# A third buffer for evacuated projection tiles, later head transposes in layer two, and a new order in the first seven-product pair

## The reference

```
h += 0.5 * g1 * SwiGLU_1(mod(norm(h)))
h += g2 * W_out [ A window attention | B global attention with QK norm | C 2-D Fourier ] (mod(norm(h)) W_in)
h += 0.5 * g3 * SwiGLU_2(mod(norm(h)))
```

## Time and profile before

| what | value |
|---|---|
| median of 3 runs | 2603.0 us (2598.9 to 2603.01) |
| the profiled execution's own time | 2601.57 us |
| its span in the trace | 2599.5 us |
| TensorE busy | 2514.5 us, 97% |
| VectorE busy | 1948.2 us, 75% |
| ScalarE busy | 1149.9 us, 44% |
| GpSimd busy | 788.7 us, 30% |

### The profile page before, as it was taken

The page is one execution under the profiler, slowest core; times in us unless marked ns, Lnnn a source line. Parts: engine busy times, 40 slices in busy tenths (PEclk is TensorE's granted clock), DMA queues, the critical chain, the costliest instruction groups (busy, mean ns, idle before and its releaser), DMA issues.

```text
span 2599.5 us, 40233 instructions
## 1 busy us (share of the span) xinstructions
PE 2514.5 (97%) x14986; PEld 2308.1 (89%) x14986; DVE 1948.2 (75%) x3213; ACT 1149.9 (44%) x2131; POOL 788.7 (30%) x614
## 2 busy tenths in 40 slices
PE   7999999999988999999999999999999999899998
PEld 4999999988777899999999899999997787899997
DVE  5888788766498488788755888887567596877776
ACT  5533433443376262433444624333444474544443
POOL 1222121224187231221222312221323285333332
PEclk9999999999999999999999999999999999999999
DMA  6244445214430124444312244443123431133332
GB/s 247 98 149 138 130 130 155 78 57 159 102 90 1 57 83 131 134 141 147 114 57 74 86 134 131 137 146 114 62 66 115 118 78 49 61 94 98 102 106 82
DMA packets 132001, 276.16 MB, mean 106 GB/s; under 512 B 15584, under 2 KB 35296, under 8 KB 130528
## 3 DMA queue, kind: packets, MB, share of 16 engines
q1 hardware_dynamic: 131808, 273.60, 34.1%
HBM read 260.43 MB, written 13.11 MB: 105 GB/s over the span
## 4 chain that ended last, share of the span: by engine, by line
PE 79%; DVE 12%; ACT 4%; issue 3%; DMA 1%; POOL 0%; SPq 0%; ACTq 0%; DVEq 0%; POOLq 0%
PE ring L1839 38%; PE ring L1941 21%; PE ring L1952 14%; DVE wlo L1435 2%; DVE ptl L1259 1%; DVE neg_max L1236 1%; PE row L1760 1%; ACT pth L1098 1%; PE row L1775 1%; PE ring L1795 1%; DVE xl L1546 1%; DVE tl L1345 1%; DVE t_lat L1539 1%; ACT whi L946 1%; DVE prob L1249 1%
## 5 line engine op out<-in xcount | busy, mean ns | idle before, releaser
L1435 DVE TENSOR_TENSOR wlo<-raw,whi 128x512 fp32r<-128x512 f32 (+2 forms) x672 | 512.4, 773 | 302.9 <-ACT whi L946 302.2
L946 ACT ACTIVATE whi<-raw 128x512 fp32r<-128x512 f32 (+2 forms) x672 | 399.1, 605 | 383.3 <-PE ring L1941 240.8
L1839 PE MATMUL ring<-xh,whi 128*128 128x384 f32 (+1 forms) x1280 | 411.8, 322 | 0.7 <-DVE rstd L1414 0.7
L1839 PE MATMUL ring<-xl,whi 128*128 128x384 f32 (+1 forms) x1280 | 411.4, 321 | 0.0
L1839 PE MATMUL ring<-xh,wlo 128*128 128x384 f32 (+1 forms) x1280 | 411.2, 321 | 0.0
L1839 PE MATMUL ring<-th,whi 128*128 128x384 f32 (+1 forms) x960 | 313.6, 327 | 14.1 <-DVE acc L1300 8.4
L1839 PE MATMUL ring<-th,wlo 128*128 128x384 f32 (+1 forms) x960 | 312.1, 325 | 0.0
L1839 PE MATMUL ring<-tl,whi 128*128 128x384 f32 (+1 forms) x960 | 311.9, 325 | 0.0
L636 POOL TENSOR_TENSOR raw<-raw,s_two 128x512 f32<-128x512 f32 x80 | 116.2, 1452 | 618.9 <-DVE wlo L1435 577.3
L1442 DVE SCALAR_TENSOR_TENSOR ada_junk<-ada_tile,row 128x1024 bf16<-128x1024 f32 x256 | 301.5, 1215 | 0.0
L622 POOL TENSOR_TENSOR s_one<-raw 128x512 f32<-128x512 f32 x80 | 104.9, 1311 | 551.8 <-DMA raw<-w_gu 441.4
(11 more groups left out here) (218 smaller groups left out, 5489.4 us busy)
## 6 DMA issues: line engine op xcount, KB each, us to landing
raw<-w_gu SPq DMA_DIRECT2D x352, 256.0 KB, 3.1
ada_tile<-w_turned SPq DMA_DIRECT2D x130, 512.0 KB, 3.7
raw<-w_down SPq DMA_DIRECT2D x96, 256.0 KB, 3.6
raw<-w_down SPq DMA_DIRECT2D x64, 192.0 KB, 2.5
raw<-w_in SPq DMA_DIRECT2D x48, 256.0 KB, 3.4
raw<-w_down SPq DMA_DIRECT2D x64, 128.0 KB, 2.1
raw<-w_out SPq DMA_DIRECT2D x32, 256.0 KB, 8.5
ada_first<-w_first SPq DMA_DIRECT2D x4, 1536.0 KB, 13.7
```

Source lines behind the costliest of these rows:

```text
L946: act.activation(weights(q, 0, cols)[0], src[:, 0:cols], ACT.Copy).then_inc(whi_ready, 1)
L1435: dve.tensor_tensor(w_l, src[:, 0:cols], w_h.bitcast(F32), ALU.subtract).then_inc(wlo_ready, 1)
L1839: last = pe.matmul(out, w, x, start=(start and k == 0 and m == 0), stop=(k == HALF - 1 and m == 2), skip_group_check=not start)
```

## The change

Three things are done. (1) `un` becomes three buffers; the third lies in memory that the value tiles use later. ScalarE evacuates tile j before it rounds tile j - 2 (except for the last two roped tiles), and new waits on the finished rope guard the buffers on ScalarE and VectorE. (2) In layer two TensorE turns the head norms before step k = 6 and not k = 4. (3) In the first seven-product pair banks b and c change places, the third turned sum is rounded (ScalarE) and its rest taken (VectorE) later, behind the last weight splits of pair 1, and the waits of TensorE move to the blocks that need them; in the last feed-forward (`rounds_late`) the product of the pair before is rounded behind the third bank copy, and its rest taken behind one more weight split.

```diff
--- before.py
+++ after.py
@@ -299,7 +299,7 @@
         rot = sb("rot", [P, 2, SEQ], F32, work + 30720)
         ucos = sb("ucos", [P, 2, SEQ], F32, work + 34816)
         rope_tab = sb("rope_tab", [P, 2, SEQ], F32, work + 38912)
-        un = sb("un", [P, 2, TOK], F32, work + 43008)
+        un = [sb(f"un{i}", [P, TOK], F32, at_un) for i, at_un in enumerate((work + 43008, work + 46080, work + 6144))]
         uf = sb("uf", [P, 2, TOK], F32, work + 49152)
         pos_lat = sb("pos_lat", [P, 4, SEQ + 1], F32, work + 55296)
         pos_ctx = sb("pos_ctx", [P, 2, CTX + 1], F32, work + 63520)
@@ -409,7 +409,8 @@
         def pair_banks(i, w2):
-            return ring[pair_ring(i)][:, 0:w2], ring[0][:, 512:512 + w2], ring[1][:, 512:512 + w2]
+            a, low, high = ring[pair_ring(i)][:, 0:w2], ring[0][:, 512:512 + w2], ring[1][:, 512:512 + w2]
+            return (a, high, low) if i == PLAIN else (a, low, high)
         def weights(q, a, b):
@@ -432,6 +433,11 @@
             return s["sums"] + d + 1 + (KD - 1 - s["whole"] if p == 1 and d >= s["whole"] else 0)
+
+        def rounds_late(s):
+
+
+            return s["width"] == SEQ
         def even_odd(a):
@@ -705,7 +711,7 @@
                         if q >= 2:
                             pool.wait_ge(qlo_done, g - 1)
                         if width == TOK:
-                            pool.tensor_copy(roped[:, sl, SEQ:TOK], un[:, sl, SEQ:TOK])
+                            pool.tensor_copy(roped[:, sl, SEQ:TOK], un[q % 3][:, SEQ:TOK])
                         pool.tensor_tensor(rot[:, sl], rot[:, sl], rope_tab[:, 1], ALU.mult).then_inc(rope_done, 1)
                         pool.wait_ge(rope_done, 2 * g + 1)
                         pool.tensor_tensor(roped[:, sl, 0:SEQ], rot[:, sl], ucos[:, sl], ALU.add).then_inc(rope_done, 1)
@@ -782,13 +788,15 @@
                     act.activation(four[:].rearrange("p c n -> p (c n)"), bank[0][:, 0:4 * P], ACT.Copy).then_inc(four_ready, 1)
                 if j == UF[1]:
                     round_values(0)
-                if 0 <= j - 2 < ROPED:
+                if j - 2 in (ROPED - 2, ROPED - 1):
                     round_qk(j - 2)
                 act.wait_ge(piece_used, s["tile"][j] + 2)
                 if j in UF:
                     act.activation(uf[:, j % 2, 0:width], ring[j % 2][:, 0:width], ACT.Copy).then_inc(evac_done, 1)
                 else:
-                    last = act.activation(un[:, j % 2, 0:width], ring[j % 2][:, 0:width], ACT.Copy, scale=SCALE if j in QA else 1.0)
+                    if j >= 3:
+                        act.wait_ge(rope_done, 2 * (q0 + j - 3) + 2)
+                    last = act.activation(un[j % 3][:, 0:width], ring[j % 2][:, 0:width], ACT.Copy, scale=SCALE if j in QA else 1.0)
                     if j not in (KB,) + QB:
                         last.then_inc(evac_done, 1)
                     else:
@@ -798,6 +806,8 @@
                     if j == QB[2] + 1:
                         head_std(QB[2])
                         act.preload_act_table(ACT.Exp)
+                if 0 <= j - 2 < ROPED - 2:
+                    round_qk(j - 2)
             round_values(1)
         def act_fourier(act, layer, between):
@@ -826,6 +836,7 @@
             end = stages[n + 1]["first"] if n + 1 < len(stages) else len(plan.pieces)
             w2, done = width // 2, t_before(n)
             shift = MODC * layer + (6 if s["kind"] == "ffn2" else 0) * KD
+            round_late = rounds_late(s)
             def ahead(q):
@@ -877,11 +888,11 @@
             ahead(q)
             round_turned(0)
             ahead(q + 1)
-            round_turned(2)
             round_turned(1)
             plain_silu(1)
             ahead(q + 2)
             ahead(q + 3)
+            round_turned(2)
             open_pair = 1
             for unit in s["units"][PLAIN:]:
                 if len(unit) == 2:
@@ -904,15 +915,17 @@
                 if k > 0:
                     act.wait_ge(comb_done, 3 * k)
                 act.activation(m1[:, 0:w2], a_bank, ACT.Copy).then_inc(copy_done, 1)
-                if open_pair is not None:
+                if open_pair is not None and not round_late:
                     round_product(open_pair)
-                open_pair = i
                 ahead(q + 1)
                 act.wait_ge(piece_used, q + 2)
                 act.activation(m5[:, 0:w2], c_bank, ACT.Copy).then_inc(copy_done, 1)
                 ahead(q + 2)
                 act.wait_ge(piece_used, q + 3)
                 act.activation(u2[:, 0:w2], a_bank, ACT.Copy).then_inc(copy_done, 1)
+                if open_pair is not None and round_late:
+                    round_product(open_pair)
+                open_pair = i
                 if i == PLAIN:
                     round_turned(3)
                 ahead(q + 3)
@@ -1146,14 +1159,16 @@
                     if b == 0:
                         dve.wait_ge(qkg_ready, 1)
                     dve.wait_ge(head_spread, b + 1)
-                    dve.scalar_tensor_tensor(out=un[:, sl, 0:width], in0=un[:, sl, 0:width], scalar=qkg[:, kq:kq + 1],
+                    dve.scalar_tensor_tensor(out=un[j % 3][:, 0:width], in0=un[j % 3][:, 0:width], scalar=qkg[:, kq:kq + 1],
                                              in1=side[:, 0:width], op0=ALU.mult, op1=ALU.mult).then_inc(unorm_done, 1)
                     dve.wait_ge(unorm_done, b + 1)
                 dve.wait_ge(evac_done, e0 + j + 1)
                 if j == 0:
                     dve.wait_ge(tab_loaded, 16 * (layer + 1))
-                dve.stream_shuffle(rot[:, sl], un[:, sl, 0:SEQ], [i ^ 16 for i in range(32)])
-                dve.tensor_tensor(ucos[:, sl], un[:, sl, 0:SEQ], rope_tab[:, 0], ALU.mult).then_inc(rot_done, 1)
+                if q0 + j >= 2:
+                    dve.wait_ge(rope_done, 2 * (q0 + j - 2) + 2)
+                dve.stream_shuffle(rot[:, sl], un[j % 3][:, 0:SEQ], [i ^ 16 for i in range(32)])
+                dve.tensor_tensor(ucos[:, sl], un[j % 3][:, 0:SEQ], rope_tab[:, 0], ALU.mult).then_inc(rot_done, 1)
             def head_reciprocal(j):
@@ -1331,7 +1346,7 @@
                 parts = t_parts(s)
                 for p, (t1, c, a, b) in enumerate(parts):
-                    dve.wait_ge(thi_done, 4 * done + len(parts) * (0, 2, 1, 3)[x] + p + 1)
+                    dve.wait_ge(thi_done, 4 * done + len(parts) * x + p + 1)
                     v = t1.rearrange("p k (b e q) -> p k b e q", e=2, q=P)
                     src = (v[:, 0:HALF, :, 0], v[:, HALF:KD, :, 1], v[:, 0:HALF, :, 1], v[:, HALF:KD, :, 0])[x]
                     if x == 3:
@@ -1358,11 +1373,11 @@
             turned_sum(2)
             rest_turned(0)
             ahead(q + 1)
-            rest_turned(2)
+            rest_turned(1)
             ahead(q + 2)
-            rest_turned(1)
             product_rest(1)
             ahead(q + 3)
+            rest_turned(2)
             open_pair = 1
             for unit in s["units"][PLAIN:]:
                 if len(unit) == 2:
@@ -1395,10 +1410,12 @@
                 if i == PLAIN:
                     turned_sum(3)
                 ahead(q + 1)
-                if open_pair is not None:
+                if open_pair is not None and not rounds_late(s):
+                    rest_product(open_pair)
+                ahead(q + 2)
+                if open_pair is not None and rounds_late(s):
                     rest_product(open_pair)
                 open_pair = i
-                ahead(q + 2)
                 if i == PLAIN:
                     rest_turned(3)
                 ada_slot((n, *unit))
@@ -1630,6 +1647,11 @@
             blocks = 6 if x_w == TOK else 4
             e0 = W_IN_TILES * layer
+            def spread_at(layer):
+
+
+                return KD // 2 if layer < DEPTH - 1 else KD - 2
+
             def head_squares(j):
                 b, width = 4 * layer + j - KB, w_in_width(layer, j)
@@ -1657,7 +1679,7 @@
                     elif half == 0:
                         pe.wait_ge(four_ready, layer + 1)
                     for m in range(n_):
-                        last = pe.transpose(bank[half][:, m * P:(m + 1) * P], un[:, b, (a + m) * P:(a + m + 1) * P], ident[:])
+                        last = pe.transpose(bank[half][:, m * P:(m + 1) * P], un[(VA + b) % 3][:, (a + m) * P:(a + m + 1) * P], ident[:])
                     last.then_inc(v_turned, 1)
             def fourier():
@@ -1695,7 +1717,7 @@
                     product_pair(s, s["tile"][0], TOK)
                 elif j > 1:
                     product(ring[j % 2], s["tile"][j], WHOLE_TILE, xh, xl, w_in_width(layer, j),
-                            k_wait=lambda k: spread_head(j - 2) if k == KD // 2 and j - 2 <= QB[2] else None)
+                            k_wait=lambda k: spread_head(j - 2) if k == spread_at(layer) and j - 2 <= QB[2] else None)
                 if j == 5:
                     pe.wait_ge(wf_loaded, 64 * (layer + 1))
@@ -1861,18 +1883,21 @@
                     pe.wait_ge(prod_done, p0 + i - 1)
```

(7 more changed lines are left out.)

## The result

The changed kernel takes **2609.55 us** (median of 7 runs, 2608.82 to 2611.12), the kernel before on the same chip 2600.76 (7 runs, 2598.30 to 2604.49). The ratio is 1.0032, 95% interval 1.0022 to 1.0042: slower by a third of a per cent, more than the 0.2% that can be told. It lies in my range (2592 to 2611), near the number of rival B (2611), and not in the case that I held likeliest. That it lies in the range at all is partly luck: I had put the change on a median of 2603.0 for the kernel before, and on the 2600.76 measured here the same range would end at 2608.8. As a difference I forecast +1.4 us and the change costs 8.8. The profiled execution of after took 2611.1 us with a span of 2609.3; before's span was 2599.5.

The account below looks back on a forecast made before the run. TensorE is busy 97% of the span, so only its idle time and slow clock can be won. 1.0 + 0.1 - 1.1 - 0.7 - 2.5 + 4.6 = +1.4 us on 2603.0 gives 2604.4 us, range 2592 to 2611.

Parts of the forecast that it names:

- rival B: Layer two's tiles four to six: each gap near 2 us costs 1.6 us more by slow clock; 2611 us, chance 0.22.
- the case that I held likeliest: Whole kernel: time the same as before within 0.2% (5.2 us), chance 0.48.
- Parts 4 and 5: Projections: third buffer removes layer two's head-norm wait, but transposes at k = 6 make the next tile's splits late; +4.6 us.
- Part 1: First seven-product pair, full-width stages: reordering moves TensorE's gap rather than removing it; +1.0, +0.1 and, first stage, -1.1 us.
- Part 2: Same reordering in the last stage, width 512: the 4.2 us gap breaks into smaller ones; -0.7 us.
- Part 3: Last feed-forward: rounding after the third copy removes TensorE's waits on that copy; -2.5 us, between 1.4 and 4.1 gained.
- rival A: Whole kernel: VectorE's queue has more slack, so the gaps close; about -13 us, 2590 us, chance 0.30.

Follow-up runs that it names:

- no_late: The changed kernel with the rounding behind the first copy again in the last feed-forward stage, not the third; 2608.94 us, ratio 1.0021.
- sum_first: k4 with VectorE's second addition ahead of the split of q+4 in the last stage's later seven-product pairs; 2598.51 us, ratio 0.9984.
- fill_hole: k4 with the third operand's rests ahead of product 1 in the three full-width feed-forward stages; 2599.91 us, ratio 0.9993.
- k4: The changed kernel with layer two's head transposes back before block four instead of six; 2599.75 us, ratio 0.9989.
- buffer_k4: The kernel before with only the third buffer and the new ScalarE order, transposes before block four; 2600.11 us, ratio 0.9991.
- after_again: The changed kernel, unedited, profiled a second time; 2610.12 us.
- k6_only: The kernel before with only layer two's head transposes moved to before block six; 2610.91 us, ratio 1.0033.

## Why the prediction was right and wrong

- **Parts 4 and 5 (forecast +4.6): right.** Measured +5.2 and +5.3, with the four gaps within 0.25 us of those written. The experiments split them: the buffer alone -2.9, block six on top of it +8.1. The clock fell behind the longest gap alone, as written, but for longer: the four gaps less before's 2.28 and 0.89 make 4.3 of the 5.2, so its fall cost some 0.9 us more than the 1.6 that I took.
- **Part 1 (+1.0, +0.1, -1.1): the mechanism right, the sizes off by up to 0.7 us.** VectorE's hole before product 1 is 2.47 us (forecast 2.5), and one whole GpSimd sum and the end of another fall in it (I had two). The pair groups give +0.4 and +0.5, -0.3 and -0.4, and in the first stage -1.8 and -0.7, where before's clock had fallen (PEclk 0.83 from 80 to 90 us) and after's had not. The wait before q+6 of the next pair, which I took to shift by 0.95 from 0.43, is 1.16; in the first stage it is 1.16 too, where I had it shrink from its 0.29.
- **Part 2 (-0.7): right, as far as the profiles tell.** -0.3 and -1.4, of which 1.1 is the difference between before's two profiles. The gap broke up before q+2, q+3, q+4 and q+6, the last at 1.97 us (forecast about 2.2).
- **Part 3 (-2.5): the step that failed.** Measured +0.9 and -0.1 for the later pair groups. I had read that the addition (L1414) ends 0.15 to 0.2 us before its use, and had set the value halfway to 4.1 nonetheless, "since splits of that piece come earlier". Almost nothing came earlier: 4.4 us of waits on the copy (no_late) stand against 3.7 on the addition (after), and no_late takes 0.6 us less, not 2.5 more. The low end of my own range (1.4), by the row that I held against rival A, was nearer, and still more than the runs show.
- **Outside the change (forecast 0): +3.0**, the clock in A to D, **and +2.4 or +1.4** ahead of the first pair group. I had priced a fall only behind gaps that the change makes. That these belong to the change is not shown.
- **Rival A's sum was wrong.** 4.8, 4.1 and 1.6, half of 8.4 and 1.6 are 16.3 us, not 13. The forecast doesn't use it.

So the forecast of +1.4 missed, by the profiles, 2.4 to 3.4 us in part 3 and 4.3 to 5.5 outside the change, less 0.6 to 1.7 won in part 1 beyond what I had; that carries it over the 0.2% line. Rival B came near the right number by other places: the clock did not fall three times in tiles four to six, but in B, C and D, where nothing was edited.

## What to carry to other kernels

When a transfer or a wait is moved later on one engine, list what else stands behind its consumer in the consumer's queue: here the weights of the next tile stood behind a norm, and moving the splits ahead of it won 2.4 us where moving the transposes two blocks later had lost 8. When the row beside a wait shows 0.2 us of room, price its removal at 0.2 us. An idle hole on VectorE in which GpSimd works may be worth nothing: here 3.1 us were lost for 2.47 won. And before a stretch's time is laid to an edit, look whether another kernel with the same instructions there has the other value.

## What was not expected of the hardware

The clock's falls come as pieces of about 1.6 us (longer in the projections of after), and whether one comes does not follow from the length of a gap alone: behind the same wait of 1.25 to 1.27 us it fell in sum_first and fill_hole and did not in k4 and buffer_k4; behind the 2.6 us of block six it did in all four profiles that had them (after, after_again, k6_only, no_late). In C it fell in k6_only and not in before behind the same wait of 1.12 us at the same 1951.90. The two profiles of one kernel agreed in A to D, but kernels with the same instructions up to there did not. Why, the runs do not show. So the total of one execution can move by 1.6 us, up or down, several times over, without an edit at that place; with a median alone these can't be told from an edit's own effect, and the cut into stretches tells them apart.
